# Odd mixer's input projection and both output projections of the first block: from whole f32 operands to high and low halves in three passes

## The reference, cut to what matters

```python
# even layer
proj = h @ in_w                                   # 1024 x 2560
u = causal_dwconv(a_val * sigmoid(a_gate), dw_w, dw_b)
u = silu(layer_norm(u, ln_g, ln_b))               # 512 wide
o = stick_breaking_attention(q, k, v)             # 512 wide
mix = concatenate([u, o], axis=-1) @ out_w        # 1024 x 1024, "evout"
x = x + g1 * mix
...                                               # rms_norm, mixture of experts
# odd layer
y_branch, x_branch = split(h @ in_w, 2, axis=-1)  # 1024 x 2048, "odin"
xc = causal_dwconv(x_branch, conv_w, conv_b)      # width 4
r = sigmoid(block_diag_linear(xc, rg_w, rg_b))
i = sigmoid(block_diag_linear(xc, ig_w, ig_b))
a = exp(8 * r * log_sigmoid(lam)); b = sqrt(1 - a * a) * i * xc
hseq = associative_scan(a, b)
mix = (gelu(y_branch) * hseq) @ out_w             # 1024 x 1024, "odout"
x = x + g1 * mix
```

## Time and profile before

| what | value |
|---|---|
| median of 3 runs | 2074.93 us (2072.07 to 2081.14) |
| profiled execution | 2072.63 us, span 2070.8 us |
| mean granted TensorE clock | 0.953 |
| PE, DVE, ACT busy | 91%, 53%, 37% of the span |
| end of even mixer and `out0` | 184 to 234 us |
| `odin` x branch, gates, y branch | 541.7 to 613.5 us |
| `out1` | 616.2 to 650.2 us |

### The profile page before, as it was taken

One profiled execution on the slowest core, in us unless ns is written; L12 is line 12 of the kernel. 1 busy time (PEld: TensorE's weight loads), 2 busy tenths in 40 slices (PEclk: granted clock), 3 DMA queues, 4 the chain that ended last, 5 costly groups with the idle time before them and its releaser, 6 DMA issues.

```text
span 2070.8 us, 24420 instructions
## 1 busy us (share of the span) xinstructions
PE 1876.0 (91%) x9900; PEld 1328.4 (64%) x9900; DVE 1095.1 (53%) x1797; ACT 759.6 (37%) x1201; POOL 112.8 (5%) x152
## 2 busy tenths in 40 slices
PE   5988799999899899999979897999999887888997
PEld 3654555455576554547635565888888573578997
DVE  1482542233444422447457636688776655646665
ACT  1154243323242433333146533323222424644443
POOL 0590000000000000000000002000000100010000
PEclk9999999999999999999979998999999897989999
DMA  9668499999556899992210021344554031024430
GB/s 389 258 259 325 163 378 400 413 397 402 208 219 257 331 417 421 421 419 111 81 41 1 1 81 41 142 184 183 202 203 176 30 121 41 1 82 163 183 143 21
DMA packets 61849, 430.18 MB, mean 208 GB/s; under 512 B 6560, under 2 KB 9760, under 8 KB 9888
## 3 DMA queue, kind: packets, MB, share of 16 engines
q1 hardware_dynamic: 61728, 428.51, 52.3%
HBM read 427.43 MB, written 1.05 MB: 207 GB/s over the span
## 4 chain that ended last, share of the span: by engine, by line
PE 72%; DVE 15%; ACT 9%; issue 2%; DMA 1%; SPq 0%; DVEq 0%; POOL 0%; ACTq 0%
PE bank L293 15%; PE bank L1053 10%; PE bank L297 9%; PE bank L298 9%; PE bank L299 9%; PE bank L1041 7%; DVE ring_halves L2378 3%; ACT work_halves L2372 2%; PE bank L332 2%; PE bank L2051 2%; ACT work_halves L973 2%; PE bank L2028 2%; DVE ring_halves L980 2%; PE bank L2390 1%; DVE work L439 1%
## 5 line engine op out<-in xcount | busy, mean ns | idle before, releaser
L297 PE MATMUL bank<-work_halves 128*128 128x512 f32 (+1 forms) x1344 | 473.1, 352 | 37.9 <-DVE ring_halves L2378 12.3
L299 PE MATMUL bank<-work_halves,ring_halves 128*128 128x512 f32 (+1 forms) x1344 | 461.2, 343 | 0.0
L297 PEld LDWEIGHTS bank<-work_halves 128*128 128x128 f32 x1344 | 258.7, 193 | 75.9 <-DVE ring_halves L2378 15.1
L298 PE MATMUL bank<-HH_halves,work_halves 128*128 128x512 f32 (+1 forms) x832 | 289.6, 348 | 0.0
L299 PEld LDWEIGHTS bank<-work_halves,ring_halves 128*128 128x128 f32 x1344 | 258.7, 192 | 29.0
L1053 PE MATMUL bank<-ring,work 128*64 128x512 f32 x1024 | 261.2, 598 | 0.4 <-ACT work_halves L1236 0.4
L2378 DVE TENSOR_TENSOR ring_halves<-ring,work_halves 128x2048 fp32r<-128x2048 f32 x72 | 164.5, 2287 | 54.2 <-ACT work_halves L2372 54.2
L293 PE MATMUL bank<-HH,ring 128*128 128x256 f32 x768 | 176.7, 390 | 16.1 <-DVE HH L518 6.6
L293 PEld LDWEIGHTS bank<-HH,ring 128*128 128x128 f32 x768 | 148.6, 195 | 49.4 <-issue 18.6
L298 PEld LDWEIGHTS bank<-HH_halves,work_halves 128*128 128x128 f32 x832 | 161.8, 194 | 20.2 <-issue 2.2
L298 PE MATMUL bank<-work_halves 128*128 128x512 f32 (+1 forms) x512 | 172.0, 336 | 0.0
(11 more groups left out here) (303 smaller groups left out, 2602.4 us busy)
## 6 DMA issues: line engine op xcount, KB each, us to landing
ring<-in_ws_dram SPq DMA_DIRECT2D x381, 1024.0 KB, 7.6
work<-in_ws_dram SPq DMA_DIRECT2D x23, 1024.0 KB, 9.4
con<-in_con_dram SPq DMA_DIRECT2D x1, 1204.0 KB, 15.7
XX<-in_xT_dram SPq DMA_DIRECT2D x1, 1024.0 KB, 11.6
XX<-in_cT_dram SPq DMA_DIRECT2D x1, 1024.0 KB, 15.3
out_dram<-XX SPq DMA_DIRECT2D x1, 1024.0 KB, 4.8
par<-in_par_dram SPq DMA_DIRECT2D x1, 338.0 KB, 2.9
con<-in_con_dram SPq DMA_DIRECT2D x1, 128.0 KB, 2.7
```

Of the source, the lines that this page charges most:

```text
L297: pe.matmul(out, l[0], r[0], start=start, stop=False)
L298: pe.matmul(out, l[0], r[1], start=False, stop=False)
L299: return pe.matmul(out, l[1], r[0], start=False, stop=stop)
```

## The change

Three projections go from 16 whole f32 matmuls for each chunk to 48 float32r matmuls. ACT gets, for each of the 16 chunks, a copy of 128 x 2048 (`split_act`, high half, into free work memory), and DVE a subtraction of the same size (`split_dve`, low half, written over the chunk in the ring). For the activations ACT gets 24 copies of 128 x 256 (8 tiles in each of the three places) and DVE 24 subtractions. PE waits for the low halves in place of the load. `out0` takes its tiles in the order 4, 5, 6, 7, 0, 1, 2, 3. The list of loads stays as it was. The diff at its core:

```diff
 # Even.act, behind the attention's loop
                         act.activation(O1[:, 4 + c, :], bank[self.o.of["o", c][0]][:, 0:256], ACT.Copy).then_inc(st.act("evicted", ("o", c)), 1)
+                        st.wait_ge(act, "evicted", ("o", c))
+                        self.next.high_x(act, 4 + c)
                 for s in range(34, 38):
                     self.bg.act(act, s)
+                for j in range(4):
+                    self.next.split_act(act, j)
                 st.wait_ge(act, "centred")
                 act.activation(sqw[:, 0:4, :], self.cv, ACT.Square).then_inc(st.act("centred squares"), 1)
...
                     act.activation(O1[:, c, :], self.cv[:, c, :], ACT.Silu, scale=par_("lng", c), bias=par_("lnb", c)).then_inc(st.act("u", c), 1)
+                    st.wait_ge(act, "u", c)
+                    self.next.high_x(act, c)
 # Even.dve
                 dve.tensor_tensor(cv, cv, bc(mu, 4), SUB).then_inc(st.dve("centred"), 1)
+                for c in range(4):
+                    self.next.low_x(dve, 4 + c)
+                for j in range(2):
+                    self.next.split_dve(dve, j)
                 st.wait_ge(dve, "root")
...
+                for c in range(4):
+                    self.next.low_x(dve, c)
+                for j in range(2, 4):
+                    self.next.split_dve(dve, j)
 # Out
+            def split_act(self, act, j):
+                key = (self.key, j)
+                loaded(act, key)
+                act.activation(r_(self.high[j]), ring_of(key), ACT.Copy).then_inc(self.st.act("high", j), 1)
+
+            def split_dve(self, dve, j):
+                w = ring_of((self.key, j))
+                self.st.wait_ge(dve, "high", j)
+                dve.tensor_tensor(r_(w), w, r_(self.high[j]).bitcast(F32), SUB).then_inc(self.st.dve("low", j), 1)
...
-                    loaded(pe, key)
+                    st.wait_ge(pe, "low", j)
                     for m in range(2):
-                        t = mms(pe, b[:, 256 * m:256 * m + 256], [(w[:, k, P * m:P * m + P], O1[:, k, :]) for k in range(8)])
+                        for n, k in enumerate(self.rows):
+                            st.wait_ge(pe, "xl", k)
+                            c = slice(P * m, P * m + P)
+                            t = mm3(pe, b[:, 256 * m:256 * m + 256], (wh[:, k, c], wl[:, k, c]), (xh[:, k, :], xl[:, k, :]), n == 0, n == 7)
 # Odd.act
                 act.activation(sm(3), sm(2), ACT.Exp, scale=-1.0).then_inc(st.act("e"), 1)
+                self.split_act(act, 0)
+                for k in range(8):
+                    norm2.st.wait_ge(act, "h", k)
+                    act.activation(self.X[0][:, k, :], H1[:, k, :], ACT.Copy).then_inc(st.act("xh", k), 1)
+                self.split_act(act, 1)
+                self.split_act(act, 2)
                 for j in range(4, 8):
                     c = 2 * (j % 4)
+                    if j == 4:
+                        self.split_act(act, 3)
                     st.wait_ge(act, "used", ("odin", j))
                     act.activation(self.xp[:, c:c + 2, 3:259], self.pv(j), ACT.Copy).then_inc(st.act("evicted", ("p", j)), 1)
+                    if j < 7:
+                        self.split_act(act, j)
+                self.split_act(act, 7)
...
                     act.activation(self.yb[:, 2 * j:2 * j + 2, :], self.pv(j), ACT.Gelu_apprx_tanh).then_inc(st.act("evicted", ("p", j)), 1)
+                    out1.split_act(act, j)
+                for n in range(8):
+                    st.wait_ge(act, "o", n)
+                    out1.high_x(act, n)
 # Odd.dve
+                for k in range(8):
+                    st.wait_ge(dve, "xh", k)
+                    dve.tensor_tensor(self.X[1][:, k, :], H1[:, k, :], self.X[0][:, k, :].bitcast(F32), SUB).then_inc(st.dve("xl", k), 1)
+                    if k == 0:
+                        self.split_dve(dve, 0)
+                self.split_dve(dve, 1)
+                self.split_dve(dve, 2)
                 st.wait_ge(dve, "e")
...
+                self.split_dve(dve, 3)
                 for n in range(8):
+                    if n % 2 and n > 1:
+                        self.split_dve(dve, 4 + n // 2 - 1)
                     st.wait_ge(dve, "evicted", ("p", 4 + n // 2))
...
+                self.split_dve(dve, 7)
...
                 st.wait_ge(dve, "b")
+                st.wait_ge(dve, "used", self.keys[7])
                 for n in range(8):
+                    if n % 2:
+                        out1.split_dve(dve, n // 2)
                     dve.tensor_tensor_scan(xc[:, n, :], self.rr[:, n, :], self.ii[:, n, :], 0.0, MUL, ADD).then_inc(st.dve("scan", n), 1)
                     st.wait_ge(dve, "scan", n)
                     st.wait_ge(dve, "evicted", ("p", n // 2))
                     dve.tensor_tensor(O1[:, n, :], xc[:, n, :], self.yb[:, n, :], MUL).then_inc(st.dve("o", n), 1)
+                    if n > 0:
+                        out1.low_x(dve, n - 1)
+                out1.low_x(dve, 7)
```

More of the change, by code:

```diff
@@ L806, in __init__ @@
                 self.ro = Rota(list(range(6)))
+                self.high = [work[:, WORK - CW * (i + 1):WORK - CW * i] for i in (3, 2, 1, 0)]
+                self.X = [k8(halves["HH"][:, :], 512)[:, :, 256 * i:256 * i + 256] for i in range(2)]
                 for j in range(4):
@@ L2657, in build @@
         out0 = Out("out0", "evout", mods[0], first, 38)
+        even.next, out0.rows = out0, (4, 5, 6, 7, 0, 1, 2, 3)
         norm1 = Norm("norm1", "ffng0", mods[0], 24, out0.st, first, range(42, 46))
@@ L2663, in build @@
         out1 = Out("out1", "odout", mods[1], second, 12)
+        out1.rows = range(8)
         norm3 = Norm("norm3", "ffng1", mods[1], 24, out1.st, second, range(16, 20))
@@ L2729, in tensor_program @@
             odd.pe(pe, norm2)
-            out1.pe(pe, odd.wait_o)
+            out1.pe(pe)
             norm3.pe(pe)
```

45 lines of the change are left out of this document (31 added, 14 removed).

## The result

The changed kernel takes 2088.74 us (median of 8 runs, 2085.62 to 2094.11), the kernel before 2076.33 us beside it (8 runs, 2071.07 to 2081.14). The ratio is 1.0068, with a 95% interval from 1.0057 to 1.0080: 14.1 us more, between 11.8 and 16.6. The profiled execution took 2090.53 us, span 2088.7.

What follows compares the result with a forecast made beforehand. Serial ACT and DVE chains that PE waits for at three places were taken as the bound. `out0` +4.9 and the odd layer +10.3 sum to 15.2 on 2072.63, giving 2087.8, stated as 2089 us; range 2078 to 2098.

Steps and rivals of the forecast that it cites:

- What PE gains: In the three projections, a chunk of 48 float32r records takes 5.78 us against 6.91: 1.13 less, 18.1 for 16 chunks.
- the four-pass estimate: PE's chunk if true FP32 takes four passes: three passes take 5.18 us, saving 1.73; end estimate about 10 us lower.
- What a split costs: On ACT and DVE, 2048-column copies take 1.9 us and subtractions 2.3; a tile's chain grows by about 0.9.
- First place, `out0`: Even output projection: ACT's square waits behind the split of evout 3, +9.8; the place costs +4.9 us in all.
- the one for chunk 0: In `out0`, chunk 0 ends at 215.5 and not at 207.2: +8.3 us.
- bound (+7.5): Cost of `out0` if two high halves also lie on the attention's chain and the clock is half through the first chunk.
- Second place: Odd input projection: PE starts 5.5 us later, first chunk ends +4.0, but odin 3 is used at 608.5, not 612.5.
- DVE's splits make the last gates +0.7 late: Odd input projection: DVE's splits among the taps end at 582.3, so the last gates end 0.7 us late.
- Third place, `out1`: Odd output projection: late splits and low halves hold PE, chunk 0 ends +13.8 us; +10.3 since the odd mixer's start.
- the third rival: Clock stays half longer in `out0`, first odd chunk and `out1`: 4 to 6 us more, 2096 to 2102; chance 0.10.
- PE alone sets the time: Whole kernel: splits fill idle ACT and DVE time, all 18.1 us come off, 2055 to 2057; chance 0.05.
- The wait for evout 3: In `out0`; the rival said it does not bite: `out0` gains 6.6, sum +3.7, 2076 to 2079 us; chance 0.15.

Runs made afterwards that it cites:

- square_before_splits: Changed kernel with ACT's square behind the first weight split in the even layer, evout 3 split last, DVE's splits reordered: 1.0025 of the kernel before.
- one_split_behind: Changed kernel with only the fourth weight split on ACT, of evout 3, moved behind the Silus in the even layer: 1.0056 of the kernel before.
- out1_halves_first: Changed kernel; at `out1` ACT does high halves after two weight splits, DVE three of its splits behind the last low half: 1.0026 of the kernel before.
- both_orders: Changed kernel with the new orders of square_before_splits and out1_halves_first together: 0.9984 of the kernel before.
- y_splits_behind_taps: both_orders with DVE's weight splits of odin 1, 2 and 3 moved behind the eight groups of taps: 0.9982 of the kernel before.
- all_orders: both_orders, both_k_outer and y_splits_behind_taps together: 0.9966 of the kernel before.
- pe_kept_busy: Changed kernel with added matmuls of constants at four places where PE waits, 20 ahead of the variance: 1.0098 of the kernel before.
- both_k_outer: both_orders, with PE doing both output groups of chunk 0 as each tile comes, in both output projections: 0.9959 of the kernel before.
- pe_kept_busier: pe_kept_busy with 27 added matmuls ahead of the variance, not 20, and 26 between tiles of the odd chunk 0, not 14: 1.0073 of the kernel before.

## Why the prediction was right, point by point

The prediction said 2089 us; the result is 2088.74, and the sum of +15.2 stands against +14.1 by the runs and +16.0 by the three columns. That the two times agree to a quarter of a microsecond is luck: `out0` was 1.5 too small and the odd layer 0.6 too large, the base that I took for the kernel before (2073.8) was not its median beside the result (2076.33), and executions of one kernel scatter by more. What the prediction had right is the mechanism at the first and third place and the size of both within 2 us.

- **What PE gains.** Chunk steps 5.75 and 6.90: 1.15 less, where I took 1.13. Right, and the four-pass estimate (5.18 a chunk) was not.
- **What a split costs.** The copies took 1.91 and the subtractions 2.28 to 2.29. Right.
- **First place, `out0`: +4.9, measured +6.4.** The square came 10.1 later (9.8), the root 11.8 (11.5). The term that was too small is the one for chunk 0, +8.3 against +9.8: half clock in chunk 0 too, from 213 to 216 us. The 27 records took 4.5 us there and not 3.2. I had the half clock as a bound (+7.5) and not in the sum. That the wait was the cause is shown by square_before_splits and, in size, by one_split_behind.
- **Second place.** The first odd chunk's eviction moved by 3.1 us (from 551.20 to 561.73, with the norm 7.4 late), where I said 4.0, and the first scan by 0.65 where I said 1.2. The step was half right. That odin 3 sets the first scan holds: in the changed kernel PE runs from 554.3 us, where the first x chunk starts, to the last y chunk with one gap of 0.2 us, and the scan waited 2.84 us for it. That DVE's splits make the last gates +0.7 late does not: PE's last gate began 47.17 us behind the norm's reciprocal, 47.24 before. PE's own sum, 3.1 - 3.4, gives it, and DVE added the 0.2; those 0.7 are the error in the scan. In the two executions with late loads above, DVE's chain was the later one, by 1.0 and 1.4 us.
- **Third place, `out1`.** Chunk 0's eviction +13.1 relative to the norm, said +13.8; all of the odd layer +9.7, said +10.3. The low halves took 16.0 us from first to last (said 15 to 16), DVE idle ahead of them 2.61 us. out1_halves_first shows that the order made it.
- **Slips in the working.** With four passes the estimate would not have been 10 us lower: the sum counts the chunk step only where PE sets the time, and not in all 16 chunks. 560.6 + 15.1 + 6.6 and half a microsecond is 582.8, 0.4 behind the 582.4 and not 0.7. Four to 6 us above the forecast is 2093 to 2095, not the 2096 to 2102 of the third rival. And 10.4 us was far too coarse for what can be told from no change: the interval of the result is 4.8 us wide.
- **The rivals.** That PE alone sets the time is refuted: ahead of both output projections ACT and DVE hold PE longer than before. The wait for evout 3 did bite. The clock stayed half longer than in my sum in one of the places that the third rival names, chunk 0 of `out0`, where it cost about 1.2 us; that rival's size (4 to 6 us) did not come.

## What to carry to other kernels

Sixteen chunks that became 1.15 us cheaper on the busiest engine made this kernel slower, since the work that makes them cheaper was queued ahead of the instructions that PE waits for. Before adding work to an engine with idle time, find the next instruction in its queue that another engine waits for, and the last load that the new work needs; put the work behind it. Here the same work in another order turned +14 us into -3, and with PE taking tiles as they come -8.5. Where two chains end together, as in the x branch here, shortening one is worth nothing.

## What the runs showed of the hardware

- Loads of 1 MB queued together landed evenly here: three of ACT's splits began 2.49 us apart, each behind its landing, and the next 4.97 later with a background chunk between. So a landing could be read from the load's place in the queue; no run changed the queue, and with the same list the first of them landed 1.3 us later behind the attention's end in one_split_behind.
- The 32 records of a whole f32 chunk took 7.14 us behind a wait of 2.62 us and 9.47 behind one of 7.99, with a granted clock of 0.50 from 620 to 626 us. Here time won on PE ahead of a wait was paid back in part by its clock.
- Executions of one kernel scatter by 10 us and more (2068 to 2081 for the kernel before, with a mean granted clock of 0.956 in the fastest and 0.949 in the slowest), and the profiled ones differ in stages that no edit touches: 3.6 us in the experts, 5 in the rest. For the experts the traces show where. The windows from 8 to 16 and from 24 to 32 us behind the norm's reciprocal, in both_orders (experts 301.13) and in y_splits_behind_taps (304.26):

```profile
238.70:246.70 8.00, 6.80 (x47) 4.97 (x47) 7.17 (x22) 4.71 (x8) 0.00 (x0) 0.79 0.00 0
254.70:262.70 8.00, 6.62 (x38) 6.41 (x39) 5.21 (x13) 6.01 (x10) 0.00 (x0) 0.70 0.47 165
```

```profile
240.10:248.10 8.00, 8.00 (x44) 6.71 (x48) 7.03 (x21) 4.35 (x7) 0.00 (x0) 0.54 0.00 0
256.10:264.10 8.00, 4.66 (x22) 4.69 (x23) 7.18 (x17) 3.69 (x6) 0.00 (x0) 0.50 0.17 62
```

  In the slower one the granted clock is lower in the routing, and the experts' load into the work memory is issued 31.35 us after the reciprocal and not 29.29; from 40 to 200 us the DMA engines are all but full and the clock is 1.00 in both. The first of these windows shows 0.52 to 0.54 in out1_halves_first, all_orders and pe_kept_busy too (304.2 to 304.6 us), 0.63 and 0.66 in both_k_outer and pe_kept_busier (302.6), and 0.79 in the kernel before and the changed one (301.0 to 301.1). So 2.1 of the 3.1 us are there when that load starts. What makes an execution take the one course or the other, and whether the clock makes all of the scatter, is open.
